# Where the second block's attention begins: moving two unfoldings, two gates and one low part

## The reference

```python
for l in range(DEPTH_2):                     # 2 layers
    h = _rms_norm(x, norm_g[l])
    p = h @ w_in[l]
    c_q, c_kv, k_pe, z_a, u_f, z_f, g_a, g_f = _split_in(p)
    o_a = _mla_branch(c_q, c_kv, k_pe, ...)  # bidirectional attention, softmax over 512 keys
    y_a = (o_a * jax.nn.silu(z_a)) @ w_attn_proj[l]
    y_f = (_fourier_branch(u_f) * jax.nn.silu(z_f)) @ w_fourier_proj[l]
    m = sigmoid(g_a + b_merge[l, 0]) * y_a + sigmoid(g_f + b_merge[l, 1]) * y_f
    x = x + m @ w_out[l]

def _fourier_branch(u):                      # 4 groups of 128 features
    ug = u.reshape(b, s, N_FOURIER_GROUPS, FOURIER_GROUP_DIM)
    return jnp.real(jnp.fft.fft2(ug, axes=(1, 3), norm='ortho')).reshape(b, s, FOURIER_WIDTH)
```

## Time and profile before

| | |
|---|---|
| median of 3 runs | 1461.88 us (1461.09 to 1464.12) |
| the profiled execution | 1465.13 us, of which the span of the core's instructions 1463.3 us |
| granted TensorE clock, mean over the span | 0.998 |
| TensorE busy | 1444.7 us of the span (99%) |
| VectorE, ScalarE, GpSimd busy | 799.3, 622.8, 368.4 us |

### The profile page before, as it was taken

The page is one execution under the profiler, slowest core; times in us unless marked ns, Lnnn a source line. Parts: engine busy times, 40 slices in busy tenths (PEclk is TensorE's granted clock), DMA queues, the critical chain, the costliest instruction groups (busy, mean ns, idle before and its releaser), DMA issues.

```text
span 1463.3 us, 18815 instructions
## 1 busy us (share of the span) xinstructions
PE 1444.7 (99%) x7077; PEld 1210.2 (83%) x7077; DVE 799.3 (55%) x1321; ACT 622.8 (43%) x971; POOL 368.4 (25%) x368
## 2 busy tenths in 40 slices
PE   9999999999999999999999999999999999999997
PEld 7888888888888888888888888888888888888886
DVE  5648864334543433344478795444447879543444
ACT  5436862233322313224434695333333479522332
POOL 2004521102000000001307785211110778500011
PEclk9999999999999999999999999999999999999999
DMA  5664333323223323223242113233223211323221
GB/s 193 86 125 118 103 109 100 102 87 119 94 87 100 102 88 105 93 86 111 60 124 59 31 49 108 86 89 113 96 84 116 62 33 45 109 87 115 87 88 58
DMA packets 160498, 135.65 MB, mean 93 GB/s; under 512 B 35929, under 2 KB 153953, under 8 KB 160417
## 3 DMA queue, kind: packets, MB, share of 16 engines
q1 hardware_dynamic: 160256, 134.50, 31.0%
q10 hardware_dynamic: 160, 0.07, 0.0%
HBM read 124.26 MB, written 2.92 MB: 87 GB/s over the span
## 4 chain that ended last, share of the span: by engine, by line
PE 93%; DVE 3%; ACT 1%; issue 1%; POOL 1%; DVEq 0%; ACTq 0%; POOLq 0%
PE G L1936 75%; PE S L1918 4%; PE G L1918 3%; PE T L2027 2%; PE G L2051 2%; PE G L2058 2%; PE G L2148 1%; DVE sq L1530 1%; PE G L2317 1%; PE G L1984 1%; PE G L2102 1%; POOL t L853 1%; ACT w L1052 1%; PE G L2283 0%; PE G L2154 0%
## 5 line engine op out<-in xcount | busy, mean ns | idle before, releaser
L1936 PE MATMUL G<-gx,w 128*128 128x512 f32 x2928 | 671.9, 390 | 1.3 <-DVE w L1392 1.3
L1936 PEld LDWEIGHTS G<-gx,w 128*128 128x128 f32 x2928 | 548.9, 188 | 116.9 <-DVE w L1392 1.7
L1392 DVE TENSOR_TENSOR w<-raw,w 128x2048 fp32r<-128x2048 f32 (+2 forms) x110 | 252.6, 2297 | 223.7 <-ACT w L1052 223.7
L1052 ACT ACTIVATE w<-raw 128x2048 fp32r<-128x2048 f32 (+1 forms) x112 | 209.9, 1874 | 126.4 <-PE G L1936 109.6
L1936 PE MATMUL G<-kvb,w 128*128 128x512 f32 x960 | 218.4, 389 | 0.0
L1936 PEld LDWEIGHTS G<-kvb,w 128*128 128x128 f32 x960 | 180.2, 188 | 37.4
L853 POOL TENSOR_TENSOR t<-t,rden 128x512 f32<-128x512 f32 (+2 forms) x128 | 109.1, 854 | 113.1 <-DVE rden L1536 111.2
L895 POOL TENSOR_TENSOR t<-sig 128x512 f32<-128x512 f32 x24 | 35.4, 1473 | 335.4 <-DVE sig L1604 335.4
L1667 DVE TENSOR_TENSOR x<-G,x 128x512 f32<-128x512 f32 x56 | 38.6, 689 | 115.3 <-PE G L1936 115.3
L993 POOL TENSOR_TENSOR sumsq_f<-sumsq_f,sq_f 128x512 f32<-128x512 f32 x7 | 9.1, 1301 | 333.4 <-ACT sq_f L1082 333.4
L1936 PE MATMUL G<-m,w 128*128 128x512 f32 x384 | 87.4, 389 | 0.0
(11 more groups left out here) (249 smaller groups left out, 1791.6 us busy)
## 6 DMA issues: line engine op xcount, KB each, us to landing
raw<-in_w_in SPq DMA_DIRECT2D x98, 512.0 KB, 7.5
raw<-in_w_up SPq DMA_DIRECT2D x32, 512.0 KB
raw<-in_w_down SPq DMA_DIRECT2D x32, 512.0 KB
raw<-in_w_out SPq DMA_DIRECT2D x24, 512.0 KB
raw<-in_w_attn_proj SPq DMA_DIRECT2D x8, 512.0 KB
raw<-in_w_fourier_proj SPq DMA_DIRECT2D x8, 512.0 KB
biasb<-bias_rows SPq DMA_DIRECT2D x24, 128.0 KB
xin<-in_x SPq DMA_DIRECT2D x4, 512.0 KB, 6.8
```

The costliest lines, as they stand in the source:

```text
L1052: nc.scalar.activation(cut(K.w[:, j % 2, 0, 0:n]), cut(K.raw[:, j % 2, 0:n]), ACT.Copy).then_inc(K.w_hi, 1)
L1392: nc.vector.tensor_tensor(cut(K.w[:, s, 1, 0:n]), cut(K.raw[:, s, 0:n]), cut(K.w[:, s, 0, 0:n]).bitcast(F32), ALU.subtract).then_inc(K.w_l ...
L1936: mm = nc.tensor.matmul(b[:, :], w(p, k), x(q, k), start=(k == i == 0), stop=(k == kts - 1 and i == len(PASSES) - 1))
```

## The change

Four things are moved, in both layers; no arithmetic is added or dropped.

- ScalarE: `odd_part(1)` goes ahead of `fourier_hi(0)`, and `odd_part(2)`, which came behind `fourier_hi(1)`, now comes first, with `fourier_hi(1)` behind `odd_part(3)`.
- VectorE: the low part of group 0 (`branch_lo(0)`) is gone; GpSimd makes it (`branch_low(l, 0, 0, TT)`, one instruction over 512 columns) ahead of its first probabilities.
- VectorE: `unfold(2)` (called `second`) stood ahead of `qk_lo` of head 1, before the loop over the steps; it now stands in the loop at n = 1, behind `low(0)`.
- GpSimd: the gates of groups 2 and 3 come behind the probabilities of steps 2 and 4 (before: ahead of step 0 and behind step 3), and the low parts move back by a step or two. The gate of group 2 waits for a total of `tile_out` that is higher by 2.

```diff
-GATE_AT = 3
-LOW_AT = {2: (1, 0), 4: (1, 1), 6: (1, 2), 7: (1, 3), 8: (2, 0), 10: (2, 1), 11: (2, 2), 12: (2, 3),
+GATE_AT = {2: 2, 4: 3}
+LOW_AT = {3: (1, 0), 6: (1, 1), 7: (1, 2), 8: (1, 3), 10: (2, 0), 11: (2, 1), 12: (2, 2), 15: (2, 3),
...
-            if A.kind == "L" and n == GATE_AT:
-                fourier_gated(A.layer, TT - 1)
+            if A.kind == "L" and n in GATE_AT:
+                fourier_gated(A.layer, GATE_AT[n])
...
-        pool.wait_ge(K.tile_out, Num(G_L + fourier_tile(grp, "seq"), (l, GL)).value())
+        pool.wait_ge(K.tile_out, Num(G_L + fourier_tile(grp, "seq") + (2 if grp == 2 else 0), (l, GL)).value())
...
-        for grp in range(TT - 1):
+        for grp in range(2):
             fourier_gated(l, grp)
-            for i in range(2 * grp, 2 * grp + 2) if grp < 2 else ():
+            for i in range(2 * grp, 2 * grp + 2):
                 slab_low(l, i)
+        branch_low(l, 0, 0, TT)
         probabilities(Heads(K, "L", l))
...
-                if grp >= 2:
-                    fourier_hi(grp - 2)
...
             elif grp < TT - 1:
                 odd_part(grp)
+                if grp == 1:
+                    fourier_hi(0)
                 gi += 1
-        attention(heads, first=lambda: odd_part(TT - 1), branch=fourier_hi)
+        def fourier_end():
+            odd_part(TT - 1)
+            fourier_hi(1)
+        attention(heads, first=fourier_end, branch=fourier_hi)
...
         for n in range(AHEAD):
             if n == 2 and A.kind == "L":
-                second()
                 qk_lo(A, 1)
                 rden(n - 1)
...
         for n in range(total):
+            if n == 1 and A.kind == "L":
+                second()
             if n == 2 and third is not None:
                 third()
...
-                if grp == 2:
-                    branch_lo(0)
```

More of the change, by code:

```diff
@@ L97 @@
 BRANCH_AT = {5: 2, 9: 3}
-GATE_AT = 3
-LOW_AT = {2: (1, 0), 4: (1, 1), 6: (1, 2), 7: (1, 3), 8: (2, 0), 10: (2, 1), 11: (2, 2), 12: (2, 3),
-          15: (3, 0), 16: (3, 1), 18: (3, 2), 19: (3, 3)}
+GATE_AT = {2: 2, 4: 3}
+LOW_AT = {3: (1, 0), 6: (1, 1), 7: (1, 2), 8: (1, 3), 10: (2, 0), 11: (2, 1), 12: (2, 2), 15: (2, 3),
+          16: (3, 0), 18: (3, 1), 19: (3, 2), 20: (3, 3)}
 HEAD_SQUARES = ((0, 1), (2, 3), (4, 5), (6, 7), (), (), (), ())
@@ L947, in fourier_gated, with branch_low @@
             pool.wait_ge(K.pool_ok, Num(4, (l, 12)).value())
-        pool.wait_ge(K.tile_out, Num(G_L + fourier_tile(grp, "seq"), (l, GL)).value())
+        pool.wait_ge(K.tile_out, Num(G_L + fourier_tile(grp, "seq") + (2 if grp == 2 else 0), (l, GL)).value())
         nc.gpsimd.tensor_tensor(K.z[:, grp, :], K.unfolded[:, grp % 2, :], K.z[:, grp, :], ALU.mult).then_inc(K.fz_ok, 1)
-    def branch_low(l, grp, i):
-        c, h = slice(i * P, (i + 1) * P), Num(H_L + 16 + grp, (l, HL))
+    def branch_low(l, grp, i, n=1):
+        c, h = slice(i * P, (i + n) * P), Num(H_L + 16 + grp, (l, HL))
         pool.wait_ge(K.split_hi, (h + 1).value())
-        mm = nc.gpsimd.tensor_tensor(K.u[:, 1, grp, c], K.z[:, grp, c], K.u[:, 0, grp, c].bitcast(F32), ALU.subtract)
-        if i == TT - 1:
-            mm.then_inc(K.split_lo, 1)
+        low = nc.gpsimd.tensor_tensor(K.u[:, 1, grp, c], K.z[:, grp, c], K.u[:, 0, grp, c].bitcast(F32), ALU.subtract)
+        if i + n == TT:
+            low.then_inc(K.split_lo, 1)
     def slab_low(l, i):
@@ L1840, in program_vector @@
                     head_roots()
-        def branch_lo(grp):
-            lo(K.u[:, 1, grp, :], K.z[:, grp, :], K.u[:, 0, grp, :], h + 16 + grp)
         def unfold(grp, of):
```

## The result

The changed kernel took 1467.52 us (median of 8 runs, 1464.29 to 1470.12), the kernel before on the same chip 1462.85 us (8 runs, 1460.64 to 1464.35). The ratio is 1.0029, with a 95% interval of 1.002 to 1.0038: slower, by 0.29%. On the median that the prediction started from, 1461.88, this ratio gives 1466.1. The profiled execution took 1467.65 us, with a span of 1465.9 and a mean granted clock of 0.997.

A forecast was written before the change was run, and what follows sets the result against it. TensorE, busy 99%, was taken as the bound, with holds of 2.3 us a layer to win. 1461.9 plus 2.8 for the new wait (1.37 and 1.45 by layer) plus 1.0 for one clock fall gave 1465.7 us, range 1463.2 to 1467.4.

The forecast's parts named there:

- Odd half first: Second half of group 3's dim product: TensorE's hold for the unfolding goes, gaining 0.85 us in layer 1, 0.77 in layer 2.
- T(0) not held: First transposes: with no gate ahead of GpSimd's first probabilities, T(0) starts at 831.14 unheld, gaining 0.55 us.
- The count: Scores(4) wait on tile_out for the moved unfolding: TensorE waits some 2.9 us, scores(4) at 834.48, 1.53 us late.
- What is won back: Loop behind scores(4): T(2) 1.09 us late, T(5) 1.37 late through VectorE's reciprocal; layers lose 1.37 and 1.45 us.
- The gates: Gates of groups 2 and 3 on GpSimd cost nothing, covered by TensorE's lateness; uncovered, up to 0.8 us a layer.
- The clock: Behind the scores(4) wait the clock likely halves for 3.4 us, costing 1.0 us net in a layer; lower bound nothing.
- the nearer end of the case: Likeliest case, new wait plus clock fall in one or both layers, 1465.7 to 1466.7, chance 0.53; nearer end, one fall: 1465.7.
- Rival C: Scores(4) wait absent; 0.85 us won, 0.73 lost in VectorE's work before T(5): 1461.7 us, no change; chance 0.08.
- Rival D: Holds at the dim product and T(0) go, nothing replaces them: faster, 1460.2 or 1459.1 us; chance 0.03.
- the part on T(5): At T(5), VectorE's unbroken work up to its reciprocal sets the time; reciprocal at 841.15, 1.37 us late, T(5) with it.

The follow-up runs named there:

- e5: Kernel before with only ScalarE's new order (odd halves ahead of high parts), low part of group 0 still on VectorE; one run, 1465.53 us.
- e6: Kernel before with only the low part of group 0 moved to GpSimd, behind the gate of group 2; one run, 1467.47 us.
- e1: Changed kernel with unfold(2) back in its old place ahead of head 1's low parts, gate's total restored; 1462.44 us, ratio 0.9993.
- e9: Kernel before with ScalarE's new order and GpSimd's first two weights' low parts moved behind the gate of group 1; one run, 1464.70 us.
- e2: Changed kernel with only totals changed: scores(4) no longer wait for unfold(2), head 2's turning does; 1463.37 us, ratio 1.0001.
- e4: Changed kernel with nine extra unused 96x512 matmuls ahead of scores(4), filling the wait; 1463.83 us, ratio 1.0016.
- e3: Kernel before with only unfold(2) moved into the loop, plus the gates and low parts that must follow; 1469.04 us, ratio 1.0044.
- e8: Changed kernel with unfolding 2 in its old place, unfolding 3 moved from n = 2 to n = 5, gate and totals adapted; 1460.99 us, ratio 0.9983.
- e7: Kernel before with only the gates of groups 2 and 3 and the low parts moved on GpSimd; one run, 1464.77 us.
- e10: Changed kernel run again unaltered for a second trace; one run, 1465.71 us.
- e11: Changed kernel run again unaltered for a third trace; one run, 1467.01 us.

## Why the prediction was right

It said slower, by the wait of scores(4) with a fall of the clock in one layer or both, and put 1465.7 us. The ratio gives 1466.1 on the same median; the median of the runs, 1467.52, lies 0.1 over the top of the range, on a chip where the kernel before took 0.97 us more than the 1461.88 that I started from. Inside the traces the two layers grew by 1.40 + 2.55 = 3.95 us, put at 2.8 + 1.0 = 3.8.

- **Odd half first.** Put at 0.85 and 0.77, with the unfolding between 821.8 and 822.3. It started at 821.77, which is 822.02 in the times of before, and the hold is gone. Its worth can't be had alone (e5 and e6 both lose), but e1 keeps 0.87 and 0.71 of the 1.28 and 1.14 that it and the next term win by T(0). Of the 1.09 us of the low part that stood ahead of the unfolding 0.69 are work, and the rest was a wait for GpSimd, which I hadn't seen (e9).
- **T(0) not held.** Put at 831.14, came at 831.01, which is 831.26 in the times of before: by T(0) 1.28 us are won where 1.4 was put. GpSimd's low part took 1.29 (put at 1.4).
- **The count.** Put: scores(4) at 834.48 behind 2.9 us. Came at 834.31 behind 2.70 of idle time, which is 2.9 counted as the prediction did, from 0.41 after the start of T(0). Each step was there: `low(0)` 832.75 (833.01), unfolding 833.36 (833.62), and 0.95 from the unfolding's start to TensorE (0.86). e2 shows that the count, and not the unfolding's late place, is what costs.
- **What is won back.** T(2) 836.23 (836.42), T(5) 842.27 (842.48), reciprocal 840.94 (841.15). From `low(0)` on the times are 0.17 to 0.26 early, and this trace is 0.25 ahead at the first mark. The sum for the layer without a fall, 1.37, came as 1.40, 1.41 and 1.38 in three traces; for the second, put at 1.45, e4 has 1.47.
- **The gates.** Nothing, under cover of TensorE's lateness: no hold at T(3). e2 takes the cover away and shows 0.57 at T(3), the prediction said up to 0.8.
- **The clock.** Put at 1.0 net for a layer, or 2.4 for the layer as a whole. The second layer grew by 2.55, 2.33 and 2.55, which is 0.9 to 1.1 over the 1.47 of e4. That one layer and not both would pay was taken as the nearer end of the case and not worked out, so that part of the number is luck: with a fall in both layers the prediction's sum is 1466.7. The rule of the Trainium skill that stood there (TensorE: Matmul & The Clock Gate, "HAM oscillation — how this bites in real kernels") was read too widely in the prediction: it speaks of longer waits than the 2.7 us here, so by its words neither layer had to pay. The traces differ from it as it is written: the clock fell behind 2.7 us in one layer of the changed kernel, in both of e3, and behind 1.63 us in e6.
- **Rival C** took the loss of 0.73 us of VectorE's idle time for real, and it is: e2, where the wait is away, gains 0.14 us in the first layer and loses 0.01 in the second, put at a gain of 0.1. **Rival D** is e1, at the lower of its two prices: 0.87 and 0.71 a layer, put at 0.85 at least. The upper, 1.4, overlooked what the part on T(5) had said, that VectorE sets the time there.

What stays open: why the first layer escapes the fall, and whether the gain of e8 could be had with `unfold(2)` in the loop as well, which was not tried.

## What to carry to other kernels

A counting semaphore that several readings share makes whoever waits for a total wait for everything that stands ahead in the reader's order. Before moving a reading in such a list, write down for each waiter which instruction completes its total, then and now; here a move of 0.8 us of work put a round trip of 2.7 us in front of TensorE, and changing the totals alone took it out again. And a hold that is removed is worth only what the next engine lets through: T(0)'s 0.56 us gave 0.15 by themselves (e7), and of the 1.28 us won by T(0) in e1 only 0.87 were left behind T(5). With VectorE's work ahead of step 5's reciprocal shortened (e8) the layer won 1.48.

## What the runs showed of the hardware

**VectorE and GpSimd keep each other waiting.** The subtraction of 128x512 with both inputs in SBUF takes 0.69 us with GpSimd idle (e9), 1.09 when it slips between two GpSimd instructions, the second of which then takes 1.73 in place of 1.29 (before), and 1.83 and 1.68 when it arrives behind the start of one (e5). The Trainium skill says so (SBUF — State Buffer, "Who interferes with whom"): a VectorE instruction with two SBUF inputs and a GpSimd instruction that reads SBUF block each other, by order of issue. The traces agree: each of the two has waited for the other. My expectation for e5 had left this out and was 0.6 us a layer too small.

**The clock falls behind waits of quite different length, and not always.** It fell behind 1.63 us (e6, first layer), 2.0 (e5, first) and 2.7 (the changed kernel, second; e3, both), and stayed behind 1.64 (e6, second), 1.85 (e5, second) and 2.7 (the changed kernel, first, three times). Within one execution of e6 the same wait, 1.63 and 1.64 us, had both outcomes. Where it fell it cost 0.9 to 1.1 us in the changed kernel, 1.12 in e6 (1.58 less 0.46) and 1.44 in e5 (2.66 less 1.22, of which 0.15 is the longer hold). In e1 and e6 the clock is at half over the last 8 us of the span too, behind a wait of 1.57 us that the other traces have as well; there the last 16 transposes take 2.90 us and not 2.45.

**The start.** Ten of thirteen traces have the first fall, which begins at 8.6 to 10.7 us; three (e5, e10, e11) don't, with the same wait of 1.88 us ahead of it. In these three TensorE is 2.6 to 2.7 us earlier at the first mark than in the trace before, where the others lie within 1.0. The fall makes 1.4 to 1.7 of that: from the end of the wait of 1.88 to the first mark they have 810.9 to 811.0 us, the others 812.4 to 812.5. The rest was won ahead of the end of that wait. That is the size of the spread within one kernel: the runs of the kernel before with a mean clock of 1.0 took 1460.6 to 1462.2 us, those at 0.998 took 1461.8 to 1465.3, 18 of 21 of them over 1463. The end adds to it: from the start of the last transposes' group to the end of the span before has 1463.3 - 1449.9 = 13.4 us, the changed kernel 1465.9 - 1453.7 = 12.2 in its first trace and 13.8 in its third. Together the two are about as large as the 4 us between the two groups of e4's runs, but no trace of its faster group was taken, so this is a likely cause and not a shown one. The intervals of the ratios reach 1.3 to 2 us to either side, so whole runs can't rank kernels that lie 1 us apart; the marks of the changed kernel's three traces agree to 0.03 us in the first layer and 0.2 in the second.
